# The weight buffers of a split-float32 decoder trunk are moved 64 bytes along each partition

## The chip, the cores and the metric

The kernel runs on one core of one Trainium2 chip. The metric is the device time of one execution in microseconds (us), as the median of several runs. Lower is better.

## The reference, cut to what matters

A two-layer decoder trunk over one sequence of 512 tokens of 1024 features, in float32. Each layer is a half-step SwiGLU block, a token mixer beside an attention over 256 memory tokens, and a second half-step SwiGLU block:

```
x = x + 0.5 * swiglu_ffn(rmsnorm(x, ffn1_norm[i]), ffn1_w_in[i], ffn1_w_out[i])
h = rmsnorm(x, mix_norm[i])
mk, mv = split(mem_n @ mem_w_kv[i])
z = h @ w_in                    # layer 0: HGRN2, layer 1: chunked gMLP; plus 4 query heads
x = x + concat([o_mix, o_mem]) @ w_out
x = x + 0.5 * swiglu_ffn(rmsnorm(x, ffn2_norm[i]), ffn2_w_in[i], ffn2_w_out[i])
```

Nearly all arithmetic is in the products with weight matrices: 1024 x 5632 into and 2816 x 1024 out of each of the four SwiGLU blocks, 1024 x 5120 into each mixer, 2048 x 1024 and 3072 x 1024 out of them, and 1024 x 2048 per layer for the memory's keys and values.

## The kernel before, in words

**Split operands.** Every weight product is done in the rounded type float32r with both operands split in a top and a rest: `x*w` is computed as `x_hi*w_hi + x_lo*w_hi + x_hi*w_lo`, three matmuls in place of one. Activations lie in `h_hi`, `h_lo` (8 blocks of 128 features by 512 tokens) and `act_hi`, `act_lo` (24 such blocks, in the same place as the scratch `work`).

**Units and lanes.** The weights come in units of 8 blocks of 128 x 128 (512 KB, a few of 6 blocks). There are four lanes; unit n uses lane n mod 4, so the weight buffers are `[128, 4, 8, 128]`, which is 16 KB per partition. A unit goes through four steps:

1. SyncE (`load`, L889 to L893; also L223, L909 and L942) waits until the unit that used the lane before is done and issues one DMA of the unit into `raw[:, j]`. For most loads each partition gets eight pieces of 512 bytes.
2. ScalarE (`hi`, L1442 to L1444) rounds `raw` into `w_hi`.
3. VectorE (`lo`, L1172 to L1174) writes `w_lo = raw - w_hi`. `w_lo` lies in the very place of `raw`: L136 allocates `raw` and gives it free at once, and `w_lo` is the next allocation.
4. TensorE (`unit`, L1005 to L1015) runs 24 matmuls: for each of the 8 blocks, three with a 128 x 128 weight block as the stationary operand and a block of 512 tokens as the moving one (256 tokens for the memory's keys), summed in one PSUM bank.

Each engine's queue is an order written out by hand. ScalarE and VectorE do the `hi` and `lo` of a unit two units ahead of TensorE, in between the work on results (SiLU, product, split of the next activations).

**Where the weights move instead.** For the memory's values (L1056 to L1058), gMLP's v part (L766 to L768) and the last phase (`Final`, L249 to L251) the activations are stationary (128 tokens) and the weights are the moving operand, 256 or 512 columns wide; the last phase and the v part load them in pieces of 2 KB.

**Phases.** Keys and values of the memory (32 units, some 100 us), then for each layer ffn_in (44 units), ffn_out (24), mixer in (40), mixer out (16 or 24), ffn_in, ffn_out.

**Addresses.** Buffers are laid out in the order of the `sb(...)` calls, beginning 128 bytes past a multiple of 2048: `ident`, `ones`, `q_row` (512 bytes each) and `small` (384) fill up exactly to the next multiple, so that `x` and all after it begin at multiples of 2048 bytes: `x` at 18432, `raw` and `w_lo` at 34816, `w_hi` at 51200, `rstd` at 67584. Every block of 512 tokens, and every lane, then begins at a multiple of 2048 as well, and every 128 x 128 weight block at a multiple of 512.

Of the kernel before, what the change touches and what calls it, by code (L numbers as in the profile page):

```python
# [33 lines left out]
P = 128  # L34
# [3 lines left out]
T = 512  # L38
# [45 lines left out]
def hybrid_trunk(nc, a, out):  # L84
# [34 lines left out]
    with ExitStack() as ctx:  # L119
        def sb(name, shape, dt=F32):  # L120
            return ctx.enter_context(nc.sbuf_tensor(name, shape, dt))
# [11 lines left out]
        small = sb("small", [P, 96])  # L133
        x = sb("x", [P, DB, T])

        with nc.sbuf_tensor("raw", [P, LANES, KU, P], F32) as raw:  # L136
            pass
        w_lo = sb("w_lo", [P, LANES, KU, P], F32R)
        w_hi = sb("w_hi", [P, LANES, KU, P], F32R)
        rstd = sb("rstd", [P, T])  # L140
        sq = sb("sq", [P, 2, T])
        tmp = sb("tmp", [P, 6, T])
# [1613 lines left out]
```

## Time and profile before

| | |
|---|---|
| median of 3 runs | 2362.61 us |
| lowest to highest | 2361.79 to 2364.54 us |
| profiled execution, its own time | 2362.44 us |
| profiled execution, span from first to last instruction | 2360.7 us |
| mean granted TensorE clock | 0.998 of full speed |
| TensorE matmuls busy | 2340.6 us, 99% of the span |
| VectorE, ScalarE, GpSimd busy | 51%, 31%, 11% |
| mean DMA traffic | 99 GB/s |

The span leaves out about 1.7 us of the execution's own time. PE is TensorE's matmul stream and PEld its stream of weight loads (loads of the stationary operand), which runs beside it. A matmul's busy time reaches from its start to its modelled end, and the next starts before that end: the spacing between two starts, not the duration, is what a matmul costs in a stream. A row of the timeline has the start in us, the duration in us, the engine, the line, the operation, and how many like instructions in a row were merged.

### The profile page before, as it was taken

To read this page: it belongs to the slowest core of one execution; us is meant where nothing else is said; L and a number is where in the kernel's file an instruction comes from. 1 tells how busy PE (TensorE), PEld (TensorE's weight loads), DVE (VectorE), ACT (ScalarE), POOL (GpSimd) and SP (SyncE) were. 2 spreads that over 40 slices of the span, in tenths; PEclk is the share of its full clock that TensorE was granted. 3 is DMA by queue.
4 is the path that set the end of the run, shared out by engine and by line. 5 is a ranking of instruction groups with operands and counts; after the bars stand their busy time and mean duration, and the time that the engine had idled before them with its cause. 6 is when DMAs were issued, how large, how long until landed. Compare 5 with 4: busy or idle time off the path is not lost.

```text
span 2360.7 us, 29488 instructions
## 1 busy us (share of the span) xinstructions
PE 2340.6 (99%) x10944; PEld 1943.6 (82%) x10944; DVE 1197.9 (51%) x1411; ACT 743.0 (31%) x1005; POOL 263.3 (11%) x235
## 2 busy tenths in 40 slices
PE   9999999999999999999999999999999999999998
PEld 9988888877888888888878888887788888888887
DVE  6654443446888654444445444344337644444422
ACT  4432222234444322222223223123333322322322
POOL 3400001111333420000110000120001212000000
PEclk9999999999999999999999999999999999999999
DMA  7733333332222333333333333333233233333322
GB/s 233 215 98 96 94 94 98 98 107 63 72 71 78 100 91 97 98 98 98 97 90 91 96 98 98 98 98 98 70 94 88 83 96 107 98 98 94 93 95 92
DMA packets 400691, 234.32 MB, mean 99 GB/s; under 512 B 7692, under 2 KB 386672, under 8 KB 400624
## 3 DMA queue, kind: packets, MB, share of 16 engines
q1 hardware_dynamic: 397328, 223.37, 32.1%
q0 software_dynamic: 3280, 10.02, 1.2%
q8 instruction: 46, 0.75, 0.1%
q14 instruction: 21, 0.17, 0.0%
q10 hardware_dynamic: 16, 0.00, 0.0%
HBM read 227.07 MB, written 6.29 MB: 99 GB/s over the span
## 4 chain that ended last, share of the span: by engine, by line
PE 95%; DVE 2%; ACT 1%; issue 1%; DMA 0%; POOL 0%; ACTq 0%; DVEq 0%; SPq 0%; POOLq 0%
PE acc L1012 26%; PE acc L1014 26%; PE acc L1013 26%; PE acc L766 1%; PE acc L768 1%; PE acc L767 1%; PE mix L398 1%; PE mix L385 1%; PE acc L249 1%; PE acc L251 1%; PE acc L250 1%; PE mix L250 1%; PE mix L249 1%; PE mix L251 1%; PE mix L833 1%
## 5 line engine op out<-in xcount | busy, mean ns | idle before, releaser
L1174 DVE TENSOR_TENSOR w_lo<-raw,w_hi 128x1024 fp32r<-128x1024 f32 (+1 forms) x422 | 548.3, 1302 | 658.4 <-ACT w_hi L1444 647.8
L1012 PE MATMUL acc<-h_hi,w_hi 128*128 128x512 f32 x1920 | 759.2, 395 | 7.5 <-DVE h_lo L1236 5.3
L1014 PE MATMUL acc<-h_hi,w_lo 128*128 128x512 f32 x1920 | 748.4, 390 | 0.0
L1013 PE MATMUL acc<-h_lo,w_hi 128*128 128x512 f32 x1920 | 747.9, 390 | 0.0
L1444 ACT ACTIVATE w_hi<-raw 128x1024 fp32r<-128x1024 f32 (+1 forms) x422 | 436.5, 1038 | 354.3 <-DMA raw<-in_ffn_w_out_dram 222.0
L1012 PEld LDWEIGHTS acc<-h_hi,w_hi 128*128 128x128 f32 x1920 | 361.3, 188 | 85.2 <-DVE h_lo L1236 6.6
L1013 PEld LDWEIGHTS acc<-h_lo,w_hi 128*128 128x128 f32 x1920 | 361.2, 188 | 77.0 <-issue 3.7
L1014 PEld LDWEIGHTS acc<-h_hi,w_lo 128*128 128x128 f32 x1920 | 360.9, 188 | 75.6
L1012 PE MATMUL acc<-act_hi,w_hi 128*128 128x512 f32 (+1 forms) x976 | 368.7, 378 | 2.6 <-DVE act_lo L1185 1.7
L1014 PE MATMUL acc<-act_hi,w_lo 128*128 128x512 f32 (+1 forms) x976 | 366.2, 375 | 0.0
L1013 PE MATMUL acc<-act_lo,w_hi 128*128 128x512 f32 (+1 forms) x976 | 366.1, 375 | 0.0
L1299 DVE TENSOR_TENSOR tmp<-acc,rstd 128x512 f32<-128x512 f32 x176 | 121.7, 691 | 202.6 <-PE acc L1014 202.4
L1012 PEld LDWEIGHTS acc<-act_hi,w_hi 128*128 128x128 f32 x976 | 183.7, 188 | 37.1 <-DVE w_lo L1174 2.6
L1014 PEld LDWEIGHTS acc<-act_hi,w_lo 128*128 128x128 f32 x976 | 183.7, 188 | 33.1
L1013 PEld LDWEIGHTS acc<-act_lo,w_hi 128*128 128x128 f32 x976 | 183.8, 188 | 33.0 <-issue 0.5
L1516 ACT ACTIVATE act_hi<-tmp 128x512 f32 (+1 forms) x88 | 55.6, 632 | 404.7 <-DVE tmp L1305 404.7
L1664 POOL TENSOR_TENSOR sq<-x 128x512 f32 (+1 forms) x48 | 56.8, 1184 | 1130.3 <-DVE x L1394 1128.7
L1512 ACT ACTIVATE tmp<-tmp 128x512 f32<-128x512 f32 x88 | 55.6, 632 | 255.6 <-DVE tmp L1299 255.6
L1466 ACT ACTIVATE h_hi<-tmp 128x512 fp32r<-128x512 f32 (+1 forms) x48 | 30.4, 632 | 195.3 <-DVE tmp L1232 195.3
L1310 DVE TENSOR_TENSOR act_lo<-tmp,act_hi 128x512 f32 (+1 forms) x88 | 60.6, 689 | 40.2 <-ACT act_hi L1516 40.2
L1666 POOL TENSOR_TENSOR sq<-sq 128x512 f32<-128x512 f32 x48 | 78.7, 1641 | 3.8
L1305 DVE TENSOR_TENSOR tmp<-tmp 128x512 f32<-128x512 f32 x88 | 60.9, 692 | 10.7
(214 smaller groups left out, 1779.0 us busy)
## 6 DMA issues: line engine op xcount, KB each, us to landing
raw<-in_ffn_w_in_dram SPq DMA_DIRECT2D x176, 512.0 KB, 3.7
raw<-in_ffn_w_out_dram SPq DMA_DIRECT2D x70, 512.0 KB, 4.0
raw<-in_hgrn_w_in_dram SPq DMA_DIRECT2D x40, 512.0 KB, 3.7
raw<-in_gmlp_w_in_dram SPq DMA_DIRECT2D x40, 512.0 KB, 3.6
raw<-in_mem_w_kv_dram SPq DMA_DIRECT2D x32, 512.0 KB, 4.2
raw<-in_gmlp_w_out_dram SPq DMA_DIRECT2D x24, 512.0 KB, 4.0
raw<-in_ffn_w_out_dram SPq DMA_DIRECT2D x24, 384.0 KB, 3.4
raw<-in_hgrn_w_out_dram SPq DMA_DIRECT2D x16, 512.0 KB, 4.0
```

The costliest lines, as they stand in the source:

```text
L1012: pe.matmul(bank, w_hi[:, j, i, :], hi, start=(start and i == 0), stop=False)
L1013: pe.matmul(bank, w_hi[:, j, i, :], lo, start=False, stop=False)
L1014: m = pe.matmul(bank, w_lo[:, j, i, :], hi, start=False, stop=(stop and i == last))
L1174: dve.tensor_tensor(w_lo[:, j, 0:nkb], raw[:, j, 0:nkb], f32(w_hi[:, j, 0:nkb]), ALU.subtract).then_inc(w_lo_ready, 1)
L1299: dve.tensor_tensor(tmp[:, j, :], acc[j][:], rstd[:], ALU.mult).then_inc(acc_read, 1)
L1305: dve.tensor_tensor(tmp[:, j, :], tmp[:, j, :], tmp[:, j - 1, :], ALU.mult).then_inc(prod_done, 1)
L1310: dve.tensor_tensor(act_lo[:, f, :], tmp[:, j, :], f32(act_hi[:, f, :]), ALU.subtract).then_inc(act_lo_ready, 1)
L1444: act.activation(w_hi[:, j, 0:nkb], raw[:, j, 0:nkb], ACT.Copy).then_inc(w_hi_ready, 1)
L1512: act.activation(tmp[:, j, :], tmp[:, j, :], ACT.Silu).then_inc(silu_done, 1)
L1516: act.activation(act_hi[:, 2 * it + j // 2, :], tmp[:, j, :], ACT.Copy).then_inc(act_hi_ready, 1)
L1664: pool.tensor_tensor(sq_one, x[:, m_, :], x[:, m_, :], ALU.mult).then_inc(sq_ready, 1)
L1666: pool.tensor_tensor(sq_sum, sq_sum, sq_one, ALU.add).then_inc(sq_sum_ready, 1)
```

## The change

Two buffers that nothing reads or writes are allocated: one of 64 bytes per partition before the weight buffers, and one of 2048 - 64 = 1984 bytes after them.

```
         x = sb("x", [P, DB, T])

+        sb("gap", [P, 16])
         with nc.sbuf_tensor("raw", [P, LANES, KU, P], F32) as raw:
             pass
         w_lo = sb("w_lo", [P, LANES, KU, P], F32R)
         w_hi = sb("w_hi", [P, LANES, KU, P], F32R)
+        sb("rest_of_row", [P, T - 16])
         rstd = sb("rstd", [P, T])
```

## Rows read from the trace of the kernel before

**Rows 1.** The page, parts 1 and 4: busy time, and the chain that ended last.

```profile
PE 2340.6 (99%) x10944; PEld 1943.6 (82%) x10944; DVE 1197.9 (51%) x1411; ACT 743.0 (31%) x1005; POOL 263.3 (11%) x235
...
PE 95%; DVE 2%; ACT 1%; issue 1%; DMA 0%; POOL 0%; ACTq 0%; DVEq 0%; SPq 0%; POOLq 0%
```

**Rows 2.** Waits of PE: total us, times, longest us.

```profile
PE acc L1012 <- DVE h_lo L1236: 5.3, 3, 2.2
PE acc L1012 <- DVE w_lo L1174: 2.8, 2, 2.2
```

**Rows 3.** Groups of PE by form: busy us, mean ns, idle us before.

```profile
L1012 PE MATMUL acc<-h_hi,w_hi 128*128 128x512 f32 x1920 | 759.2, 395 | 7.5 <-DVE h_lo L1236 5.3 <-DVE w_lo L1174 2.2
...
L1012 PE MATMUL acc<-act_hi,w_hi 128*128 128x512 f32 x848 | 331.5, 391 | 0.3 <-DVE act_lo L567 0.3
...
L766 PE MATMUL acc<-w_hi,h_hi 128*128 128x512 f32 x128 | 50.6, 395 | 0.0
...
L1012 PE MATMUL acc<-act_hi,w_hi 128*128 128x256 f32 x128 | 37.1, 290 | 2.4 <-DVE act_lo L1185 1.7 <-DVE w_lo L1174 0.6
L1056 PE MATMUL acc<-w_hi,act_hi 128*128 128x256 f32 x128 | 36.6, 286 | 0.7 <-ACT tmp L1476 0.7
...
L249 PE MATMUL acc<-w_hi,act_hi 128*128 128x512 f32 x88 | 35.1, 399 | 0.0
...
L398 PE MATMUL mix<-work 128*128 128x256 f32 x128 | 28.9, 379 | 0.0
L385 PE MATMUL mix<-work 128*128 128x512 f32 x64 | 28.8, 592 | 0.0
```

**Rows 4.** Timeline from 300.1 us, inside ffn_in; the last row is 51 matmuls on.

```profile
300.11 0.39 PE L1012 MATMUL acc<-h_hi,w_hi 128*128 128x512 f32 x1
300.12 0.19 PEld L1013 LDWEIGHTS acc<-h_lo,w_hi 128*128 128x128 f32 x1
...
311.67 0.39 PE L1012 MATMUL acc<-h_hi,w_hi 128*128 128x512 f32 x1
```

**Rows 5.** Timeline from 98.5 us, memory values (256 wide); the last is 19 matmuls on.

```profile
98.50 0.28 PE L1058 MATMUL acc<-w_hi,act_lo 128*128 128x256 f32 x1
...
100.78 0.28 PE L1056 MATMUL acc<-w_hi,act_hi 128*128 128x256 f32 x1
```

**Rows 6.** Timeline from 2249.8 us, last phase, moving weights; the last is 9 on.

```profile
2249.80 0.39 PE L250 MATMUL acc<-w_lo,act_hi 128*128 128x512 f32 x1
...
2251.84 0.39 PE L250 MATMUL acc<-w_lo,act_hi 128*128 128x512 f32 x1
```

**Rows 7.** Timeline of PE: two runs of attention matmuls in plain float32, merged.

```profile
493.49 3.61 PE L398 MATMUL mix<-work 128*128 128x256 f32 x16
...
508.73 3.59 PE L385 MATMUL mix<-work 128*128 128x512 f32 x8
```

**Rows 8.** Windows: PE, PEld, DVE, ACT, POOL busy (count); clock, DMA share, GB/s.

```profile
0.00:60.00 60.00, 55.88 (x449) 55.13 (x450) 37.90 (x63) 29.59 (x42) 21.95 (x38) 1.00 0.75 234
60.00:120.00 60.00, 57.03 (x439) 54.74 (x438) 37.85 (x39) 26.38 (x34) 26.29 (x33) 1.00 0.70 209
120.00:480.00 360.00, 357.80 (x1579) 296.07 (x1578) 165.95 (x182) 100.04 (x123) 22.44 (x18) 1.00 0.33 96
```

**Rows 9.** DMA: packets, MB and share of queue q1; issues with us to landing.

```profile
q1 hardware_dynamic: 397328, 223.37, 32.1%
...
raw<-in_ffn_w_out_dram SPq DMA_DIRECT2D x70, 512.0 KB, 4.0
...
raw<-in_mem_w_kv_dram SPq DMA_DIRECT2D x32, 512.0 KB, 4.2
```

**Rows 10.** Groups by form of DVE and ACT that prepare the weights.

```profile
L1174 DVE TENSOR_TENSOR w_lo<-raw,w_hi 128x1024 fp32r<-128x1024 f32 x398 | 518.9, 1306 | 584.7 <-ACT w_hi L1444 574.1 <-DMA v_scratch<-tmp 4.7
L1444 ACT ACTIVATE w_hi<-raw 128x1024 fp32r<-128x1024 f32 x398 | 416.2, 1049 | 277.0 <-DMA raw<-in_ffn_w_out_dram 144.7 <-DMA raw<-in_gmlp_w_out_dram 45.7 <-DMA raw<-in_mem_w_kv_dram 34.4
```

More of the change, by code:

```diff
@@ L134, in hybrid_trunk @@
         x = sb("x", [P, DB, T])
+        sb("gap", [P, 16])
         with nc.sbuf_tensor("raw", [P, LANES, KU, P], F32) as raw:
@@ L139, in hybrid_trunk @@
         w_hi = sb("w_hi", [P, LANES, KU, P], F32R)
+        sb("rest_of_row", [P, T - 16])
         rstd = sb("rstd", [P, T])
```

## The prediction

> **What bounds the kernel now.** I read the page's busy times and its chain first. TensorE is busy for 99% of the span and carries 95% of the chain that ended last [rows 1]. Then the waits of PE: the two largest, for `h_lo` at the start of a phase and for `w_lo`, sum to 8.1 us out of 2360.7 [rows 2]. So nothing but the spacing of matmuls matters, apart from a few us at the start, and a change can help only by making that spacing shorter, or hurt by making it longer or by letting the weights come late.
>
> The spacing is read from the timeline. From 300.11 to 311.67 us there are 51 steps of one 512-column matmul: 11.56/51 = 0.2267 us each [rows 4]. At the full clock of 2.4 GHz, which the windows grant throughout (PEclk 1.00) [rows 8], 512 columns need 213.3 ns. So each matmul costs 13.4 ns over its columns. The 256-column ones show the same surplus: 2.28/19 = 0.1200 us against 106.7 ns, so 13.3 ns [rows 5]. It is the same when the weights are the moving operand: 2.04/9 = 0.2267 us [rows 6]. It is a price per matmul, not per column.
>
> The attention's plain float32 matmuls do not pay it. Their 256 columns are spaced by (3.61 - 0.379)/15 = 0.2154 us and 512 by (3.59 - 0.592)/7 = 0.4283 us [rows 3, 7] (the last one's duration taken off the merged stretch). That is what 1.2 columns per ns would give (213.3 and 426.7 ns) and some 2 ns more. They too have a weight load for each matmul, at 2048-byte and 512-byte multiples. So what float32r pays in addition is about 13.4 - 2.1 = 11.3 ns per matmul, and it comes only where the moving operand is read at 2.4 columns per ns.
>
> In the steady stretch the weight load for the next matmul starts within 10 ns of the current matmul's start [rows 4], so TensorE fetches two SBUF operands at once, always in the same phase to each other. That is the thing this change could touch: before, both addresses are the same modulo 512; after, they differ by 64.
>
> **The change part by part.**
>
> Two allocations issue no instruction, no wait and no DMA. Instruction counts stay as they are. The two new buffers add 64 + 1984 = 2048 bytes, so `rstd` and all behind it move by a whole 2048 and keep their alignment: cost 0, since no operand but the weights changes its address modulo 2048.
>
> *Matmuls.* The rows that read weights: three lines of the 1920 with `h`, three of 848 with `act`, three of 128 in gMLP's v part, six groups of 88 in the last phase, one of them shown, 9216 of 512 columns in all; and six groups of 128 of 256 columns, 768 [rows 3]. Together 9984, and 9216 x 0.2267 + 768 x 0.1200 = 2181 us is 92% of the span. The trace of before has no float32r matmul whose operands differ in the low address bits, so the effect must be bounded. Best end: the whole surplus is a collision of the two reads and the shift removes it: 9984 x 11.3 ns = 113 us gained. Other end: reading a block that starts off a 512-byte multiple costs one more 1.2 GHz cycle (0.83 ns) of fetch: 9984 x 0.83 = 8.3 us lost. I take 0, and the reason is in the rows. Stationary blocks begin at 0, 512, 1024 and 1536 modulo 2048 in turn within a unit, while the moving block begins at 0, and all 52 starts over two units lie on one even spacing; when the roles are swapped, the spacing is the same to the last digit [rows 4, 6]. So at least the address bits from 512 up do not matter. For the lower bits, the moving operand advances through memory twice as fast as the load does (2.4 against, as I infer from the spacing of plain float32, 1.2 columns per ns). Two streams of different speed sweep past each other at all relative positions; a constant offset of 64 bytes changes which pieces meet, not how many. If the surplus is a collision at all, a shift should leave its count alone, unless the stalls happen to lock the two reads to each other.
>
> A rule bears on this, and speaks against any effect of the shift. The Trainium skill (SBUF — State Buffer, "Who interferes with whom") says that TensorE has two independent SBUF read ports, one for the moving operand and one for the weight load, and that it never waits on anyone. By that the surplus is no collision and the change is worth 0. The same notes (TensorE: Matmul & The Clock Gate, "Back-to-back issue gap") put a warm 512-column matmul at N/2.4 + 2.5, so 215.8 ns; this trace disagrees for float32r with 226.7 ns and comes near it only for plain float32's surplus. If the 215.8 were reached on all 9984, 109 us would go.
>
> *DMAs into `raw`.* 422 loads write their pieces 64 bytes past a multiple of 512. Today one packet of queue q1 takes 0.321 x 16 x 2360.7 us / 397328 = 30.5 ns of an engine, nearly all of them 512 bytes [rows 9]. The trace has no piece written at such an offset, so it costs between nothing and, if an unaligned piece is written in three parts instead of two, half as much again. Nearly all of it is covered. A load may start when the lane's last unit is done, which is three units before TensorE needs it: 3 x 24 x 0.2267 = 16.3 us, against 4.0 + 1.05 + 1.31 = 6.4 us of landing, rounding and subtracting [rows 9, 10]. Ten us of slack and a DMA share of 0.33 hide any such cost [rows 8]. In the memory phase the lead is 3 x 24 x 0.1200 = 8.6 us against 4.2 + 1.05 + 1.31 = 6.6, so 2 us of slack, and the DMA share is 0.75 and 0.70 [rows 8]. There a packet must grow by about a third to bind. I take 0.
>
> *ScalarE and VectorE.* `hi` and `lo` read and write the shifted buffers, 422 times each, at 1.05 and 1.31 us. Their bounds are the same: nothing, or a cycle or so per instruction. They are busy 31% and 51%, and VectorE spends 574 us waiting for ScalarE ahead of `lo` alone, so the cover is wide [rows 1, 10]. Cost 0.
>
> **Sum.** 2362.44 us of the profiled execution plus 0. That execution is 0.17 us under the median of the runs, which is nothing; I forecast the median, 2362.6 us. About 0.2%, or 4.7 us, is what a measurement can tell from no change here.
>
> **The rivals.**
>
> *The surplus is a collision and the shift breaks it, wholly or in part.* For it: the surplus is the same per matmul whatever its width, which fits one weight load per matmul, and plain float32, which reads its moving operand at half the rate, has hardly any. Against it: the argument of the two speeds above, and the one spacing that all four offsets and the swapped roles share. Wholly removed, 2362 - 113 = 2249 us, spacing 215 ns; half removed 2306 us, spacing 221 ns. Chance 0.20, about half of it for each.
>
> *Slower: the unaligned writes fill the DMA engines in the memory phase.* The mechanism is the 512-byte piece that now straddles a boundary. It decides from the point where a packet takes a third more, because the share 0.75 then reaches 1. If a packet takes half as much again, the share would be 0.75 x 1.5 = 1.12 in the first 60 us and 0.70 x 1.5 = 1.05 in the next, so those stretch by 60 x 0.12 + 60 x 0.05 = 10 us, and the time is 2373 us. For it: the only stage where the DMA is near its bound [rows 8]. Against it: the bytes are the same. Chance 0.09. The Trainium skill (DMA: Bandwidth & Descriptors, "How a descriptor splits into AXI transactions") says of reads that a piece not starting at a 256-byte multiple is fetched from the boundary below, as more transactions; by it 512 bytes at an offset of 64 would be 3 transactions and 18 beats instead of 2 and 16, an estimate of an eighth more, which would not bind. No run here shows it yet.
>
> *Slower: TensorE's fetch of a shifted operand costs cycles.* One cycle on each matmul gives 2371 us, a surplus grown by half (5.7 ns) 2419 us. Nothing in the trace speaks for it; nothing excludes it. Chance 0.08.
>
> *The change does not do what it says*, for instance because the allocator places `w_lo` elsewhere. By the sizes it should land at 34880. It would give the same time as no effect, and its chance, 0.03, is in the likeliest case.
>
> **How the numbers follow.** No effect has 0.63, its own range 2358 to 2367 us. Faster by over 0.2% has the collision's 0.20, slower by over 0.2% has 0.09 + 0.08 = 0.17. Since the no-effect case alone is short of 8 in 10, the range goes up to 2376 us, which takes in the DMA case and the single cycle, and down to 2304, which takes in the half-removed collision. Left out are the whole removal (0.10) and a larger fetch cost (0.04).
>
> **What would show it.** Right: the 512-column spacing stays at 0.2267 us and the 256-column at 0.1200, the instruction counts are equal, and q1's share stays near 32%. The collision: a spacing under 0.2267 in the ffn_in stretch, with a window of 100 us holding more than its 441 matmuls. The DMA case: q1's share rising above 40%, PE busy in the first 120 us falling below 55.9 and 57.0 per 60 us, and new PE waits on `w_lo` there. The fetch case: a longer spacing everywhere and no new wait. A spacing that changes only where weights move, or only where they stand still, would show that the phase between the two reads matters after all.

## The result, and the profile after

The changed kernel takes 2412.48 us (median of 4 runs, 2411.39 to 2413.35) against 2362.94 us for the kernel before beside it. The ratio is 1.0209, 95% interval 1.0192 to 1.0225: slower by 49.5 us. The forecast of no effect was wrong, and the time lies outside its range.

The page of the changed kernel, parts 1, 3 and 4 (line numbers are two higher than before):

```profile
PE 2392.6 (99%) x10944; PEld 1943.0 (81%) x10944; DVE 1199.1 (50%) x1411; ACT 742.8 (31%) x1005; POOL 264.0 (11%) x235
...
q1 hardware_dynamic: 397328, 223.37, 31.4%
...
PE 94%; DVE 2%; ACT 1%; issue 1%; DMA 1%; POOL 0%; ACTq 0%; DVEq 0%; SPq 0%; POOLq 0%
```

The same instructions and, within one point in each share, the same chain; PE is busy 52 us longer, VectorE, ScalarE and GpSimd are within 2 us of before [rows 1]. No wait of PE grew by more than 0.6 us. The largest waits of PE (total us, times, longest):

```profile
PE acc L1014 <- DVE h_lo L1238: 3.9, 3, 1.7
PE acc L1014 <- DVE w_lo L1176: 3.4, 4, 2.3
```

Against 5.3 and 2.8 us before [rows 2]. The loss is in the spacing. Here is the timeline of the same stretch as [rows 4]; the last row is 51 matmuls after the first:

```profile
299.77 0.40 PE L1014 MATMUL acc<-h_hi,w_hi 128*128 128x512 f32 x1
300.01 0.39 PE L1015 MATMUL acc<-h_lo,w_hi 128*128 128x512 f32 x1
300.24 0.40 PE L1016 MATMUL acc<-h_hi,w_lo 128*128 128x512 f32 x1
...
311.67 0.39 PE L1014 MATMUL acc<-h_hi,w_hi 128*128 128x512 f32 x1
```

11.90/51 = 0.2333 us per matmul, where it was 0.2267. The steps are no longer even: in the trace's nanoseconds they alternate between 231 and 236, which is 277 and 283 cycles of 1.2 GHz (0.833 ns each), 280 in the mean, where every step had been 272. The modelled durations alternate with them, 0.40 and 0.39 us. The weight loads still start with the matmuls and have their old 188 ns. Windows of 300 to 400 us, before and after (columns as in [rows 8]):

```profile
300.00:400.00 100.00, 100.00 (x443) 82.84 (x442) 36.76 (x40) 25.17 (x30) 0.00 (x0) 1.00 0.32 94
```

```profile
300.00:400.00 100.00, 100.00 (x430) 80.59 (x429) 38.22 (x42) 25.97 (x31) 0.00 (x0) 1.00 0.31 92
```

Thirteen matmuls fewer in 100 us, at the full clock both times. The 256-column matmuls of the memory phase went the other way. Two rows of L1014 in that phase, 45 matmuls apart:

```profile
61.80 0.29 PE L1014 MATMUL acc<-act_hi,w_hi 128*128 128x256 f32 x1
...
66.91 0.28 PE L1014 MATMUL acc<-act_hi,w_hi 128*128 128x256 f32 x1
```

5.11/45 = 0.1136 us instead of 0.1200 [rows 5]. Eight of the 16 units of the keys run like this; but for the first, which has the start in it, the other keys' units and the 16 of the values come at 0.1178.

Summed over all starts of PE in both traces: steps under 0.25 us that follow a 512-column weight matmul, 2066.2 us before (9106 steps, 226.9 ns) and 2121.2 after (9108, 232.9 ns), so +55.0 us; the same of 256 columns 92.9 and 90.7, so -2.2; longer steps behind weight matmuls 53.1 and 51.9, so -1.2; all other matmuls -0.6. The sum is +51.0 us, and the spans differ by 2411.6 - 2360.7 = 50.9. The whole result is the 512-column spacing.

The loss is not the same in both roles. Where the weights stand still, these steps went from 226.9 to 233.3 ns (8209 steps); where the weights are the moving operand (gMLP's v part and the last phase), from 227.2 to only 229.0 (899 steps).

### The profile page after: what moved, and what is told of

Its sections match the earlier page's. It is cut to its first block, busy times and chain, and to the rows that moved or that the text cites. A ratio compares the mean times of both kernels' runs of the same rounds, so it can differ in the third digit from the quotient of the medians.

```text
span 2411.6 us, 29488 instructions
## 1 busy us (share of the span) xinstructions
PE 2392.6 (99%) x10944; PEld 1943.0 (81%) x10944; DVE 1199.1 (50%) x1411; ACT 742.8 (31%) x1005; POOL 264.0 (11%) x235
## 3 DMA queue, kind: packets, MB, share of 16 engines
q1 hardware_dynamic: 397328, 223.37, 31.4%
## 4 chain that ended last, share of the span: by engine, by line
PE 94%; DVE 2%; ACT 1%; issue 1%; DMA 1%; POOL 0%; ACTq 0%; DVEq 0%; SPq 0%; POOLq 0%
PE acc L1014 26%; PE acc L1016 26%; PE acc L1015 26%; PE acc L770 1%; PE acc L769 1%; PE acc L768 1%; PE mix L400 1%; PE mix L387 1%; DMA raw<-in_mem_w_kv_dram 1%; PE acc L251 1%; PE acc L253 1%; PE acc L252 1%; PE mix L251 1%; PE mix L253 1%; ACT w_hi L1446 1%
## 5 line engine op out<-in xcount | busy, mean ns | idle before, releaser
L1014 PE MATMUL acc<-h_hi,w_hi 128*128 128x512 f32 x1920 | 769.8, 401 | 6.1 <-DVE h_lo L1238 3.9
L1015 PE MATMUL acc<-h_lo,w_hi 128*128 128x512 f32 x1920 | 759.8, 396 | 0.0
L1016 PE MATMUL acc<-h_hi,w_lo 128*128 128x512 f32 x1920 | 759.6, 396 | 0.0
L1014 PEld LDWEIGHTS acc<-h_hi,w_hi 128*128 128x128 f32 x1920 | 361.4, 188 | 95.4 <-DVE h_lo L1238 5.2
L1014 PE MATMUL acc<-act_hi,w_hi 128*128 128x512 f32 (+1 forms) x976 | 373.6, 383 | 2.5 <-DVE w_lo L1176 1.2
L1014 PEld LDWEIGHTS acc<-act_hi,w_hi 128*128 128x128 f32 x976 | 183.5, 188 | 42.4 <-DVE w_lo L1176 1.9
```

The lines of the kernel that those rows point to most:

```text
L1014: pe.matmul(bank, w_hi[:, j, i, :], hi, start=(start and i == 0), stop=False)
L1015: pe.matmul(bank, w_hi[:, j, i, :], lo, start=False, stop=False)
L1016: m = pe.matmul(bank, w_lo[:, j, i, :], hi, start=False, stop=(stop and i == last))
```

## The experiments

Two kinds. Some are the whole kernel with another placement. The others, the streams, hold nothing but matmuls, nearly all float32r and in the kernel's order (`w_hi` with `h_hi`, `w_hi` with `h_lo`, `w_lo` with `h_hi`), in separate stretches of 48 to 96 that differ in placement, with only short waits between them and the other engines at rest. Streams are given by the mean step over the second half of each stretch, from the starts in the trace.

**Relative or absolute, and a stream by itself.** One stretch of the streams, where `W` and `H` are the offsets of the weight and activation buffers in elements of 4 bytes (shortened):

```
for i in range(8):
    for w, h in ((w_hi, h_hi), (w_hi, h_lo), (w_lo, h_hi)):
        pe.matmul(bank, w[:, W + 128*i : W + 128*i + 128], h[:, H + 512*i : H + 512*i + 512], ...)
```

> A stream of matmuls by itself, in the kernel's order (w_hi with h_hi, w_hi with h_lo, w_lo with h_hi, over 8 weight blocks, four times over): 25 stretches that differ in the offset of the weight buffers, of the activation buffers, in the columns and in the type. The rest of the reference is left out. Theory A (the two SBUF reads of TensorE collide, by the low address bits of one relative to the other): spacing near 0.227 us at offset 0 and near 0.233 us at 64, other offsets between 0.215 and 0.24 us; with weights and activations both shifted by 64 it is again 0.227; plain float32 stays at 0.429 at either offset. Theory B (a block that does not begin at a multiple of 512 bytes costs more to fetch by itself): 0.233 or more at every offset that is no multiple of 512, and more still when both are shifted.

Measured: 226.7 ns at offset 0, 233.3 at 64, 16 and 32, 232.4 at 128, 228.9 at 192, and 226.7 again at 256, 512 and 1024; 320 is as 64, 384 as 128, 448 as 192. With the activations shifted by 64 instead, 228.9, as weights at 192, which is the same difference modulo 256. With both shifted, 226.7. Plain float32: 429.2 ns from row to row at both offsets (a float32 matmul has two rows in the trace: 48 matmuls left 96). Two kinds of stretch more: with 128 columns the spacing is 111.7 ns at offset 0 and at 64; with only `w_hi` shifted by 64, or only `w_lo`, it is 231.1 at 512 columns. Rows of the timeline of this run, for 0 (L76), 64 (L103) and both by 64 (L211), each pair 24 matmuls apart:

```profile
38.76 0.39 PE L76 MATMUL acc<-h_hi,w_lo 128*128 128x512 f32 x1
...
44.20 0.39 PE L76 MATMUL acc<-h_hi,w_lo 128*128 128x512 f32 x1
...
107.73 0.39 PE L103 MATMUL acc<-h_hi,w_lo 128*128 128x512 f32 x1
...
113.33 0.40 PE L103 MATMUL acc<-h_hi,w_lo 128*128 128x512 f32 x1
...
380.35 0.39 PE L211 MATMUL acc<-h_hi,w_lo 128*128 128x512 f32 x1
...
385.79 0.39 PE L211 MATMUL acc<-h_hi,w_lo 128*128 128x512 f32 x1
```

5.44, 5.60 and 5.44 us per 24. So theory B falls, and of theory A this much holds: the offset of one operand to the other counts, modulo 256 bytes. DMA, ScalarE and VectorE touch nothing during these streams, and from stretch to stretch nothing changes but the address of one of TensorE's two reads, so the effect needs no other engine. The 228.9 with the activations shifted also answers to the 229.0 in the changed kernel where the weights move: there the stationary block lies 64 bytes below the moving one, modulo 256, and not above it.

**The whole kernel, everything shifted.**

```
+        sb("gap", [P, 16])
         x = sb("x", [P, DB, T])
```

> The 64 bytes are put ahead of x, so that weights, activations and all else are shifted alike. Theory A (relative address of the two reads): as the kernel before, 2362 us within 5, spacing 0.2267. Theory B (absolute alignment of each operand): at least as slow as the change, 2412 us or up to 2460.

Measured 2361.72 us beside 2362.59 for the kernel before. The timeline, last row 51 matmuls on, gives 11.56/51 = 0.2267:

```profile
299.98 0.39 PE L1013 MATMUL acc<-h_hi,w_hi 128*128 128x512 f32 x1
...
311.54 0.39 PE L1013 MATMUL acc<-h_hi,w_hi 128*128 128x512 f32 x1
```

This kernel has the weights, the DMA's target and all activations off every multiple of 128 bytes, and loses nothing. It settles the two absolute rivals at once: neither a misaligned fetch nor a misaligned DMA write costs anything here.

**Only the upper half.**

```
         w_lo = sb("w_lo", [P, LANES, KU, P], F32R)
+        sb("gap", [P, 16])
         w_hi = sb("w_hi", [P, LANES, KU, P], F32R)
+        sb("rest_of_row", [P, T - 16])
```

> Only w_hi is shifted by 64 bytes, w_lo (and the DMA's target raw) stays. Two of three matmuls of a unit read w_hi. Theory A and B alike: two thirds of the loss, near 2396 us. If the slower writes of the DMA or of VectorE were behind the loss (theory C), the time is that of the kernel before, 2362 us, since raw and w_lo are where they were.

Measured 2405.45 us: 43 of the 50 us with `raw` and `w_lo` where they were, so theory C falls. That is more than the two thirds expected. In the timeline 50 steps take 11.67 us, 0.2334 each:

```profile
299.83 0.40 PE L1015 MATMUL acc<-h_lo,w_hi 128*128 128x512 f32 x1
...
311.50 0.40 PE L1014 MATMUL acc<-h_hi,w_hi 128*128 128x512 f32 x1
```

Here the unshifted pairs do not get their old 226.7 back: the steps run 236, 235, 229, 233, 233, 234 and round again. The stream with the same shift had 231.1, so the kernel runs slower here than its stream. The cost of a matmul depends on what came before it, so it cannot be added up pair by pair.

**128 bytes.** The change with `[P, 32]` and `T - 32`.

> Both weight halves are shifted by 128 bytes in place of 64. Theory B: 2412 us as with 64. Theory A: another spacing, anywhere between 0.216 us (2250 us in all) and 0.24 us (2480 us); as with 64 only by chance.

Measured 2411.32 us, as with 64 within noise, by another rhythm (229 and 237 to 238 ns by turns in ffn_in, 233.3 in the mean, where the stream had 232.4).

**Steps of 16 bytes.**

> The stream of matmuls by itself, with the weight offset in steps of 16 bytes from 0 to 256 for 512 columns, 4 and 8 bytes, and 16 to 240 for 256 columns; nothing else of the reference. Theory A (collision by the address of one read relative to the other, with a period of 256 bytes): the spacing is a function of the offset alone; 0 and 256 give 0.2267 us, 64 gives 0.2333, 192 gives 0.2289, the ones between lie between 0.22 and 0.235, and 4 and 8 bytes, inside one 16-byte line, are as 0 or as 16. If the collision can be avoided at all, some offset between 192 and 256 is below 0.2267, near 0.22. Rival (any offset off 256 costs the same extra fetch): all of 16 to 240 at 0.2333, which 192 in the first stream already speaks against.

```
offset  0     16    32    48    64    80    96    112   128   144   160   176   192   208   224   240   256
512 c.  226.7 233.3 233.3 233.3 233.3 231.9 234.2 233.3 232.4 233.3 233.3 230.0 228.9 231.9 233.3 226.7 226.7
256 c.  (120) 118.4 118.5 117.8 117.8 118.8 117.4 120.0 118.6 120.0 120.0 118.0 117.8 116.7 117.8 120.0 (120)
```

(ns; those in brackets from the first streams.) At 512 columns nothing is below 226.7, so the hope of 0.22 failed, and so did "4 and 8 as 0 or 16": they gave 232.4 and 230.6, so alignment counts down to 4 bytes. At 256 columns equal addresses are not the best: 120.0 is as much as any offset gave. At 64 with 256 columns it gave 117.8 where the first streams had 113.3 for the very same placement.

**Four places for three buffers.**

> The stream by itself with w_hi, w_lo and h_lo each at 0, 64, 128 or 192 bytes (64 combinations, 512 columns), h_hi at 0; nothing else of the reference. While one matmul streams, the weights of the next are loaded, so the pairs that meet are w_hi with h_hi (twice, once across the block's end) and w_lo with h_lo. Theory A: where w_lo and h_lo are shifted alike and w_hi is at 0, 0.2267 us as unshifted; where all pairs differ by 64, 0.2333. If the phases of neighbours matter beyond the pair (theory A'), some combination falls below 0.2267, down to 0.216; if only the pairs count, none does.

Measured: 226.7 for the one combination with all at 0, and 227.7 to 235.5 for the other 63. `w_lo` and `h_lo` shifted alike by 64 gave 231.1, not 226.7, so the pairs that meet do not suffice. That `h_hi` follows `h_lo` may be the reason; no run tests it alone. Theory A in its pair form is too simple, and A', with a gain to be had, failed too.

**Narrower weight blocks.**

> The stream by itself with stationary blocks of 128, 96, 64 and 32 columns in place of 128, at offsets 0, 64 and 192; nothing else of the reference. Theory A: the surplus over 213.3 ns shrinks with the columns loaded, from 13.3 ns at 128 to some 10, 7 and 4 at offset 0, and likewise at 64 (from 20 ns). Theory B' (a fixed cost per matmul that the weight load has no part in): 13.3 ns at every width.

Measured for 128, 96, 64 and 32 columns loaded: 226.7, 230.0, 230.0, 231.7 ns at offset 0; 233.3, 228.3, 232.7, 231.1 at 64; 228.9, 233.3, 228.3, 231.7 at 192. Neither expectation holds. The surplus does not shrink with the load, and it isn't fixed. At offset 0 a smaller load makes the matmul slower, and its steps are uneven (229, 231, 232, 228 with 96 columns); why is not shown.

**Columns and distances.**

> The stream by itself with one set of 16 stationary and 16 moving blocks; nothing else of the reference. First the columns go from 512 down to 448 with all blocks at multiples of 256 bytes; then the distance of the moving blocks grows from 2048 by 16 to 240 bytes, with the stationary ones 512 bytes apart, with them growing alike, and with the moving distance held at 2096. Theory Q (a read can begin only in a time slot set by its address modulo 256 bytes, 16 slots of one 1.2 GHz cycle, so that equal addresses round the spacing up to a multiple of 16 cycles): the spacing is a staircase in the columns, 226.7 ns down to 508 columns or so, then 213.3 ns from about 506 to 476, then 200; and moving blocks 2096 bytes apart (3 slots on) come at 215.8 ns. Theory F (a fixed cost of 16 cycles per matmul when aligned): spacing falls evenly, 0.42 ns per column, 221.7 ns at 500, and no distance gives less than 226.7.

Measured for 512, 504, 500, 488, 480 and 472 columns: 226.7, 226.7, 223.3, 220.0, 216.7 and 213.3 ns. Over the columns' own time that is 16, 20, 18, 20, 20 and 20 cycles. The staircase of 16 cycles is not there (theory Q falls), and it is not 16 everywhere (F is wrong too); 512 columns with all at multiples of 256 have the least. A finer staircase shows: 510, 506 and 504 columns have the 226.7 of 512, 496 the 223.3 of 500, 464 has 210.0, all of them multiples of four cycles of 1.2 GHz. Two widths do not fit it, 508 with 228.1, which is more than 512 columns take, and 448 with 202.5. No distance of blocks gave less than 226.7; 2096 bytes gave 231.7.

**120 random placements.**

> The stream by itself, 512 columns, with w_hi, w_lo and h_lo each at an offset drawn from the 16 multiples of 16 bytes (120 draws), h_hi at 0; nothing else of the reference. If the surplus can be avoided by placement, some draw is clearly below 226.7 ns. If 16 cycles are the least (what the other streams suggest), none is, most lie between 228 and 236, and equal placement is the best there is.

Measured: none below 226.7, two at 226.7, the median 231.1, the highest 235.6. At 512 columns the kernel before had the best spacing that any of these streams found.

**240 and 192 bytes in the whole kernel.** The change with 60 and 48 elements in place of 16.

> The change with 240 bytes in place of 64: the address is no multiple of 64, 128 or 256, yet the stream by itself came at 0.2267 us there as at 0. If the stream by itself tells what the kernel does (theory A: only the pair's relative address modulo 256 counts), 2362 us within 10. If an operand off a 64-byte multiple costs anything of its own, over 2390.

> The change with 192 bytes in place of 64. The stream by itself: 0.2289 us, so 2.2 ns more on 9216 matmuls, 20 us: 2383 us. If the kernel's own stalls throw the stream into other rhythms, up to 2410.

At 240: 2415.37 us, ratio 1.0226 (1.0210 to 1.0242), where the stream had promised no loss. At 192: 2386.53 us, ratio 1.0100 (1.0081 to 1.0120), but in two groups of runs, 2382 and 2383, 2390 and 2392. Its trace shows two rhythms, 53 steps in the first stretch and 54 in the second:

```profile
299.62 0.40 PE L1014 MATMUL acc<-h_hi,w_hi 128*128 128x512 f32 x1
...
311.98 0.40 PE L1016 MATMUL acc<-h_hi,w_lo 128*128 128x512 f32 x1
...
1299.20 0.39 PE L1014 MATMUL acc<-h_hi,w_hi 128*128 128x512 f32 x1
...
1311.56 0.39 PE L1014 MATMUL acc<-h_hi,w_hi 128*128 128x512 f32 x1
```

12.36/53 = 0.2332 and 12.36/54 = 0.2289 us, with the same code and the same addresses in both. Where the weights move, 899 steps average 233.3 ns: moving weights 192 bytes up are the same difference as stationary ones 64 up. The two groups of runs are 8 us apart with one and the same program and the same granted clock (0.998), so it seems that the program alone does not fix the rhythm; only a run of the slower group has a trace.

**Does the entry choose the rhythm?** The streams again, each behind one matmul of another width:

> The stream by itself at offsets 0, 64, 192 and 240 (512 columns) and 0 and 64 (256 columns), each entered after one matmul of 512, 496, 480, 448, 384, 320, 256 or 128 columns, so with eight different phases; nothing else of the reference. Theory R (an offset allows several steady rhythms, and the entry chooses): at 240 some entries give 0.2267 us, as the stream did, and others 0.2333, as the kernel did; at 192 0.2289 and 0.2333; at 64 with 256 columns 0.1133 and 0.1178; at 0 all eight give 0.2267 and 0.1200. Theory K (the kernel's other engines make the difference): each offset has one spacing, whatever the entry.

Measured over the eight entries: at 0 always 226.7 and (but for one at 120.1) 120.0; at 64 always 233.3; at 192 always 228.9; at 240 two entries at 226.7 and six at 228.3; at 64 with 256 columns five at 113.3 and three at 117.8. Offset 240 after 512 columns (L317) and after 448 (L347), each pair 24 matmuls apart:

```profile
451.47 0.39 PE L317 MATMUL acc<-h_hi,w_lo 128*128 128x512 f32 x1
...
456.91 0.39 PE L317 MATMUL acc<-h_hi,w_lo 128*128 128x512 f32 x1
...
503.38 0.39 PE L347 MATMUL acc<-h_hi,w_lo 128*128 128x512 f32 x1
...
508.86 0.39 PE L347 MATMUL acc<-h_hi,w_lo 128*128 128x512 f32 x1
```

5.44 and 5.48 us for 24. Theory K, one spacing for each offset, falls: one placement can hold several steady rhythms, and 113.3 and 117.8 are two of them. That the entry chooses, as theory R has it, is likely but not shown, since each entry was run once in one execution. And R's numbers failed: it does not explain the kernel's 233.3 at 240, or its second rhythm at 192, which no entry produced. Whether other entries, the kernel's other work or the other distances of its buffers make those stays open.

**A version to beat both.** The weights unshifted, only the memory's activations moved:

```
-        mem_hi = act_hi[:, 0:4, :].rearrange("p b (k m) -> p (b k) m", k=2)
+        mem_hi = act_hi[:, 0:5, :].rearrange("p b t -> p (b t)")[:, 48:48 + 4 * T].rearrange("p (k m) -> p k m", m=MEM)
```

(and `mem_lo` alike.)

> The weights stay where they were before; only the memory's activations mem_hi and mem_lo, the other operand of the 768 matmuls of 256 columns, are shifted by 192 bytes, so that the weights stand 64 bytes past them modulo 256, as in the change. Theory A: the matmuls of the memory's keys (384) go from 0.1200 to about 0.1135 us, 2.5 us, those of the values (384) gain less; 512-column matmuls keep 0.2267. 2358 to 2362 us, so a little faster than both kernels, unless the loads of weights hold that stage, then 2362.

Measured 2360.49 us, ratio 0.9995, 95% interval 0.9986 to 1.0004: no gain that can be told from none. The 256-column steps average 119.5 ns instead of 121.6, which is 1.6 us over 763. Units settle at 113.3 or at 117.8, the two spacings of the streams, most of them at 117.8.

## Why the prediction was wrong

*What bounds the kernel* was right, and so was the way to read it: the spacing of 512-column matmuls decided alone.

*The step that failed* is the value taken for the matmuls, and in it this sentence: a constant offset "changes which pieces meet, not how many". It treated the two reads as streams running at fixed speeds, so that an offset could not matter. The runs show that it does: the steps settle into a rhythm that repeats, and the rhythm depends on the offset, 272 cycles when aligned, 277 and 283 by turns at 64 bytes (226.7 and 233.3 ns in the mean). The reading that fits is the prediction's own escape clause, "unless the stalls happen to lock the two reads to each other": the reads stall one another, and each next matmul starts from where the stall left it. No row shows a stall, so that part is argued. The evenness of [rows 4] was that of one rhythm, not indifference to address.

*The price per matmul* that the prediction read off the rows, 13.4 ns at 512 columns and 13.3 at 256, is not one either. In the streams at offset 0 the surplus over the columns' own time is 16.7 ns at 488 columns and 58.4 at 128, where the spacing is 111.7 ns. If a matmul with its weight load takes no less than that, which is an estimate from the 128-column streams, the 256-column ones (106.7 ns of columns) could never have gained the whole 11.3 ns; 113.3 is the least that was seen.

*The inference about high address bits* was right: what counts repeats every 256 bytes, and the rows showed offsets of multiples of 512 only. They said nothing on the low bits, and I took them to.

*The ends of that term* were the second fault. I let the collision only vanish, down to 2249 us, and for the loss took one cycle per matmul, 8.3 us, a size that no row gave and that `all64` shows to be nothing. For a surplus of unknown cause the rows gave no reason to let it fall and not rise. It went up by half, to 20.0 ns; that size stood in the text, priced at 2419 us, but under a mechanism (a costlier fetch by itself) that `all64` rules out, and with half of a chance of 0.08, and the range left it out.

*The rivals.* The DMA case did not happen: a packet of q1 costs 0.314 x 16 x 2411.6 us / 397328 = 30.5 ns, as before. PE is no less busy in the first 60 us (56.3 against 55.9). In the next 60 it is, 56.0 against 57.0, which was one of the signs named, but late weights do not show: PE's waits for `w_lo` grew by 0.8 us in the whole kernel, not by 10, and the last matmul of the memory phase starts at 109.3 us, where it started at 109.6. ScalarE and VectorE cost nothing, as forecast. These two lines answer to [rows 10]:

```profile
L1176 DVE TENSOR_TENSOR w_lo<-raw,w_hi 128x1024 fp32r<-128x1024 f32 x398 | 517.8, 1304 | 596.8 <-ACT w_hi L1446 584.4 <-DMA v_scratch<-tmp 6.7
```

```profile
L1446 ACT ACTIVATE w_hi<-raw 128x1024 fp32r<-128x1024 f32 x398 | 416.0, 1049 | 289.0 <-DMA raw<-in_ffn_w_out_dram 151.0 <-DMA raw<-in_gmlp_w_out_dram 47.5 <-DMA raw<-in_gmlp_w_in_dram 35.2
```

1304 and 1049 ns, as 1306 and 1049 before.

*The rule.* The Trainium skill (SBUF — State Buffer, "Who interferes with whom") has TensorE's two read ports independent and waiting on no one. These runs do not agree for float32r: with every other engine at rest, moving one operand's address against the other's changes the spacing from 226.7 to 233.3 ns, and up to 235.6 at other offsets. The measurement decides. For plain float32 the rule fits, 429.2 ns at either offset.

## What to carry to other kernels

Where a stream of 512-column float32r matmuls is the bound, place the stationary and the moving buffers at the same address modulo 256 bytes; all at multiples of 2048 does it. A 64-byte offset cost 2.1% of this kernel, and nothing tried was better than aligned. At 256 columns the advice does not hold: equal addresses had 120.0 ns, an offset of 64 bytes 113.3 or 117.8. A stream by itself tells that placement matters, not what the kernel will take: at 240 bytes it promised no loss, and the kernel lost 2.3%. A surplus that never varies may be one rhythm of several, and can be lost; and where a term's sign is unknown, its range must reach as far up as down.

## What the runs showed of the hardware

- The spacing of float32r matmuls depends on the address of the weight block relative to the moving block, down to 4-byte steps (at 4 bytes 232.4 ns against 226.7), and repeats after 256 bytes (226.7 at 0, 256, 512 and 1024; 233.3 at 64 and 320). Shifting both by 64 gave 226.7 again.
- It is a property of the stream, not of a pair: the same addresses ran at 113.3 or 117.8 ns (256 columns, 64 bytes), and at 226.7 or 228.3 ns in streams and 233.3 in the kernel (512 columns, 240 bytes).
- With 128 columns a float32r matmul with its own weight load took 111.7 ns, at offset 0 and at 64.
- Loading fewer stationary columns did not help at 512: 226.7 ns with 128 columns, 231.7 with 32, all aligned.
- A DMA into a buffer 64 bytes off cost nothing that could be seen: 30.5 ns per packet at either address.
- What makes one read depend on the other's address, and why the least is 16 cycles over the columns, was not found.
